# Rope scores of the decode streams in one single-pass product, keys and queries split into parts

## The reference, cut to what matters

```python
s = jnp.einsum('bqhc,bkc->bhqk', q_lat, ckv) + jnp.einsum('bqhr,bkr->bhqk', q_pe, kpe)
s = s.astype(jnp.float32) * MLA_SCALE
s = jnp.where(mask[None, None], s, jnp.finfo(jnp.float32).min)
p = jax.nn.softmax(s, axis=-1).astype(ckv.dtype)
```

## Time and profile before

| | |
|---|---|
| median of the runs | 2899.72 us |
| the profiled execution, its own time | 2900.53 us |
| its span | 2898.7 us |
| TensorE busy | 2745.8 us, 95% |
| VectorE busy | 1249.7 us, 43% |
| ScalarE busy | 888.6 us, 31% |
| GpSimd busy | 401.1 us, 14% |
| mean granted clock of TensorE | 0.981 |

### The profile page before, as it was taken

How to read it: one execution, slowest core, us unless ns; L and a number is a source line. 1 busy time by engine, 2 the same in 40 slices (tenths; PEclk the granted TensorE clock), 3 DMA queues, 4 the chain that set the end, 5 groups by cost and what they waited for, 6 DMA issues and landing times.

```text
span 2898.7 us, 45136 instructions
## 1 busy us (share of the span) xinstructions
PE 2745.8 (95%) x18648; PEld 2623.7 (91%) x18648; DVE 1249.7 (43%) x1695; ACT 888.6 (31%) x1182; POOL 401.1 (14%) x378
## 2 busy tenths in 40 slices
PE   6999999998998999999999999999989989999997
PEld 6999999895678899999989999999856888999997
DVE  3333333645765633333363323354466736332334
ACT  4221223415543422122332212233264424221222
POOL 0110011102135011001101001110122440100110
PEclk9999999999999999999999999999999999999998
DMA  3223223320015222321322222232101152222222
GB/s 112 73 62 88 82 56 89 80 53 10 18 27 97 59 73 62 89 82 56 89 59 72 66 80 79 57 100 76 27 7 31 37 102 59 72 66 80 78 58 75
DMA packets 367939, 191.19 MB, mean 66 GB/s; under 512 B 36477, under 2 KB 363472, under 8 KB 367822
## 3 DMA queue, kind: packets, MB, share of 16 engines
q1 hardware_dynamic: 363822, 179.07, 23.2%
q0 software_dynamic: 4000, 10.47, 1.4%
HBM read 183.58 MB, written 5.93 MB: 65 GB/s over the span
## 4 chain that ended last, share of the span: by engine, by line
PE 86%; DVE 6%; ACT 3%; issue 2%; POOL 2%; SPq 0%; DMA 0%; ACTq 0%; DVEq 0%; POOLq 0%
PE ps L584 25%; PE ps L586 25%; PE ps L585 25%; PE ps L819 2%; ACT w L1249 1%; PE ps L828 1%; POOL css L2467 1%; DVE w L1705 1%; PE ps L879 1%; DVE y L1794 1%; PE ps L947 1%; POOL ss L2467 1%; PE ps L861 1%; DVE at L1976 1%; PE ps L925 1%
## 5 line engine op out<-in xcount | busy, mean ns | idle before, releaser
L584 PE MATMUL ps<-xh,w 128*128 128x320 f32 x3456 | 1084.0, 314 | 56.9 <-DVE xl L1773 18.1
L585 PE MATMUL ps<-xl,w 128*128 128x320 f32 x3456 | 1077.4, 312 | 0.0
L586 PE MATMUL ps<-xh,w 128*128 128x320 f32 x3456 | 1077.3, 312 | 0.0
L584 PEld LDWEIGHTS ps<-xh,w 128*128 128x128 f32 x3456 | 657.5, 190 | 68.6 <-DVE xl L1773 25.3
L585 PEld LDWEIGHTS ps<-xl,w 128*128 128x128 f32 x3456 | 657.5, 190 | 0.3
L586 PEld LDWEIGHTS ps<-xh,w 128*128 128x128 f32 x3456 | 657.2, 190 | 0.0
L1705 DVE TENSOR_TENSOR w<-raw,w 128x2048 fp32r<-128x2048 f32 x180 | 418.5, 2325 | 426.7 <-ACT w L1249 426.7
L1249 ACT ACTIVATE w<-raw 128x2048 fp32r<-128x2048 f32 x181 | 345.2, 1907 | 483.2 <-PE ps L586 438.3
L584 PE MATMUL ps<-hh,w 128*128 128x320 f32 x1408 | 437.4, 311 | 1.0 <-DVE w L1705 1.0
L585 PE MATMUL ps<-hl,w 128*128 128x320 f32 x1408 | 435.1, 309 | 0.0
L586 PE MATMUL ps<-hh,w 128*128 128x320 f32 x1408 | 435.1, 309 | 0.0
(11 more groups left out here) (351 smaller groups left out, 2652.5 us busy)
## 6 DMA issues: line engine op xcount, KB each, us to landing
raw<-in_w_ffn_in_dram SPq DMA_DIRECT2D x178, 512.0 KB
raw<-in_w_ffn_out_dram SPq DMA_DIRECT2D x64, 384.0 KB
raw<-in_w_ffn_out_dram SPq DMA_DIRECT2D x64, 320.0 KB
raw<-in_w_in_dram SPq DMA_DIRECT2D x38, 512.0 KB
raw<-in_w_out_dram SPq DMA_DIRECT2D x16, 512.0 KB
out_dram<-xio SPq DMA_DIRECT2D x5, 512.0 KB, 3.1
xio<-in_x_prompt_dram SPq DMA_DIRECT2D x1, 2048.0 KB
y<-in_cache_ckv_dram POOLq DMA_DIRECT2D x8, 256.0 KB, 3.2
```

What stands on the lines that cost most here:

```text
L584: pe.matmul(out, wh, xh, start=first, stop=False)
L585: pe.matmul(out, wh, xl, start=False, stop=False)
L586: return pe.matmul(out, wl, xh, start=False, stop=last)
```

## The change

The rope product of the streams is computed in the 4-byte format that TensorE reads in one pass (`F32R` in the code), with keys and queries split in a high part (the value rounded to that format) and a low part (what is left). The parts stand below each other in the contracted rows, so that one product adds up three: high key times high query, low key times high query, high key times low query.

- Rows 0 to 31, 32 to 63 and 64 to 95 of KPT hold the high, the low and again the high part of the cached rope keys; QPE holds high, high and low of the queries; KN, now 96 rows, holds the new keys as KPT does.
- ScalarE, per stream: it copies the high rope keys first (`rope_hi`), then the latent keys, then copies the high part a second time, from its own result (`ct_sb`). VectorE computes the low part (`stream_rope_low`, `rope_lo`).
- ScalarE, per head: two copies of the rope queries instead of one. VectorE computes the low part (`latent_low`, `ql_lo`), and what reuses PSUM bank 2 waits for `ql_lo` instead of `ql_sb`.
- `pair_keys` and its first copy stand one step later, at 4h + 1, and on TensorE behind the transposes.
- Two zeroing instructions less per layer, since only rows 96 to 127 are left to clear. Two semaphores are merged into others (`y_stored` into `ml_stored`, `setup_ps` into `xio_ps`).

```diff
         def pair_keys(l, pair):
             if pair:
-                pe.wait_ge(*ql_sb.nth(l, 2 * pair - 1))
+                pe.wait_ge(*ql_lo.nth(l, 2 * pair - 1))
...
             pe.wait_ge(*ct_sb.nth(l, b))
+            pe.wait_ge(*rope_lo.nth(l, b + 1))
...
-            qn = QPE[0:ROPE, b, :, :].rearrange("c h t -> c (h t)")
+            qn = QPE[0:3 * ROPE, b, :, :].rearrange("c h t -> c (h t)")
...
-                if i == 0 and h % 2 and h + 1 < H:
-                    pair_keys(l, h // 2 + 1)
...
                 if n + 1 < NT:
                     attend_transpose(l, n + 1)
+                if i == 1 and h % 2 and h + 1 < H:
+                    pair_keys(l, h // 2 + 1)
...
-                run(QPE[0:ROPE, :, h, :], PS[0:ROPE, 2, P:2 * P].rearrange("p (b t) -> p b t", t=TS), ACT.Copy)\
-                    .then_inc(ql_sb.sem, 1)
+                for row in (0, ROPE):
+                    ins = run(QPE[row:row + ROPE, :, h, :], PS[0:ROPE, 2, P:2 * P].rearrange("p (b t) -> p b t", t=TS),
+                              ACT.Copy)
+                ins.then_inc(ql_sb.sem, 1)
...
+                run(KPT[0:ROPE, b % 2, 0:PAST], PS[0:ROPE, 1, :], ACT.Copy).then_inc(rope_hi.sem, 1)
                 run(CT[:, b % 2, :], PS[:, 0, :], ACT.Copy)
-                run(KPT[0:ROPE, b % 2, 0:PAST], PS[0:ROPE, 1, :], ACT.Copy).then_inc(ct_sb.sem, 1)
+                act.wait_ge(*rope_hi.nth(l, b))
+                run(KPT[2 * ROPE:3 * ROPE, b % 2, 0:PAST], KPT[0:ROPE, b % 2, 0:PAST].bitcast(F32), ACT.Copy)\
+                    .then_inc(ct_sb.sem, 1)
...
+            def latent_low(h):
+                dve.wait_ge(*ql_sb.nth(l, h))
+                V.tensor_tensor(QPE[2 * ROPE:3 * ROPE, :, h, :], PS[0:ROPE, 2, P:2 * P].rearrange("p (b t) -> p b t", t=TS),
+                                QPE[0:ROPE, :, h, :].bitcast(F32), ALU.subtract).then_inc(ql_lo.sem, 1)
...
+                if n % PT_ == 1:
+                    latent_low(n // PT_)
                 if n >= 3:
                     normalise(n - 3)
                 if n == NT - 3:
-                    V.memset(KPT[ROPE:64, :, 0:PAST], 0.0)
-                    V.memset(KPT[64:P, :, 0:PAST], 0.0)
+                    V.memset(KPT[3 * ROPE:P, :, 0:PAST].bitcast(F32), 0.0)
...
+            def stream_rope_low(b):
+                dve.wait_ge(*rope_hi.nth(l, b))
+                V.tensor_tensor(KPT[ROPE:2 * ROPE, b % 2, 0:PAST], PS[0:ROPE, 1, :],
+                                KPT[0:ROPE, b % 2, 0:PAST].bitcast(F32), ALU.subtract).then_inc(rope_lo.sem, 1)
...
+            dve.wait_ge(*kn_sb.nth(l, 0))
+            V.tensor_tensor(KN[ROPE:2 * ROPE, :], KPER[NOPE:QK, TP:T], KN[2 * ROPE:3 * ROPE, :].bitcast(F32), ALU.subtract)\
+                .then_inc(rope_lo.sem, 1)
+            stream_rope_low(0)
             stream_maximum(0)
...
                 for k in range(early):
+                    if k == early - 1 and b + 2 < NSEQ:
+                        stream_rope_low(b + 2)
                     level(m + k)
```

More of the change, by code:

```diff
@@ L185, in encoder @@
     SELG = tile(ctx, "selg", [P, 2, P])
+    s_w = ExitStack()
+    KPT = tile(s_w, "kpt", [P, 2, T], F32R)
+    s_w.close()
     GB = tile(ctx, "gb", [P, 2, T])
@@ L260, in encoder @@
     QLAT = tile(s_w, "qlat", [P, NSEQ, H, TS])
-    QPE = tile(s_w, "qpe", [P, NSEQ, H, TS])
+    QPE = tile(s_w, "qpe", [P, NSEQ, H, TS], F32R)
     CTOK = tile(s_w, "ctok", [P, TILES, KVL])
@@ L277, in encoder @@
     OLAT = tile(s_w, "olat", [P, H, P])
-    KN = tile(s_w, "kn", [ROPE, P])
+    KN = tile(s_w, "kn", [3 * ROPE, P], F32R)
     tile(s_w, "gap_mx", [P, 608])
@@ L281, in encoder @@
     s_w.close()
-    ROPET, SWAP, PAIR, KPT = UB[NOPE:P, 0, :], UB[0:QK, 1, 0:P], UB[NOPE:P, 1, P:P + ROPE], GB
+    ROPET, SWAP, PAIR = UB[NOPE:P, 0, :], UB[0:QK, 1, 0:P], UB[NOPE:P, 1, P:P + ROPE]
     SC, DROP = PB[0:NSEQ * 3, 0, :], KPER[0:MH, :]
@@ L320, in encoder @@
     setup_in = sem("setup_in")
-    setup_ps, setup_sb = sem("setup_ps"), sem("setup_sb")
+    setup_sb = sem("setup_sb")
     xio_ps, xio_sb = sem("xio_ps"), sem("xio_sb")
@@ L358, in encoder @@
     ct_ps, ct_sb = event("ct_ps", NSEQ), event("ct_sb", NSEQ)
+    rope_hi, rope_lo, ql_lo = event("rope_hi", NSEQ), event("rope_lo", NSEQ + 1), event("ql_lo", H)
     ss_ps, snm_sb, sexp_sb = event("ss_ps", NSEQ), event("snm_sb", NSEQ), event("sexp_sb", NSEQ)
@@ L395, in encoder @@
     ml_stored = sem("ml_stored")
-    y_stored = sem("y_stored")
     act_chain, dve_chain, pool_chain = sem("act_chain"), sem("dve_chain"), sem("pool_chain")
@@ L572, in _ @@
             dst = O["y_prompt"][0, t * P:(t + 1) * P, :] if t < PT_ else O["y_sample"].rearrange("b t f -> (b t) f")
-            sp.dma_start(dst, XIO[:, t, :]).then_inc(y_stored, 16)
-        sp.wait_ge(y_stored, 16 * TILES)
+            sp.dma_start(dst, XIO[:, t, :]).then_inc(ml_stored, 16)
         sp.wait_ge(stored, 16 * LAYER_STORES * LAYERS)
         sp.wait_ge(cn_stored, 32 * LAYERS)
-        sp.wait_ge(ml_stored, 256 * LAYERS)
+        sp.wait_ge(ml_stored, 256 * LAYERS + 16 * TILES)
     @block.tensor
@@ L843, in head_latents @@
             if h:
-                pe.wait_ge(*ql_sb.nth(l, h - 1))
+                pe.wait_ge(*ql_lo.nth(l, h - 1))
             if h % 2 and h > 2:
@@ L885, in pair_output @@
             pe.wait_ge(*on_sb.nth(l, 8 * pair + 7))
-            pe.wait_ge(*ql_sb.nth(l, min(2 * pair + 2, H - 1)))
+            pe.wait_ge(*ql_lo.nth(l, min(2 * pair + 2, H - 1)))
             for t in range(PT_):
@@ L909, in stream_keys @@
                 pe.wait_ge(*ct_sb.nth(l, b - 1))
+                pe.wait_ge(*rope_lo.nth(l, b))
             for k in range(4):
@@ L1189, in _ @@
         pe.transpose(PS[:, 0, 96:146], PROW[0:50, 1, :], IDENT[0:50, 0:50])
-        pe.matmul(PS[:, 1, 0:LAYERS * DK], ONES[0:1, :], HROW[:, :], start=True, stop=True).then_inc(setup_ps, 1)
+        pe.matmul(PS[:, 1, 0:LAYERS * DK], ONES[0:1, :], HROW[:, :], start=True, stop=True).then_inc(xio_ps, 1)
         pe.wait_ge(setup_sb, 1)
@@ L1557, in mla @@
             stream_keys(0)
-            run(KN[:, :], KPER[NOPE:QK, TP:T], ACT.Copy).then_inc(kn_sb.sem, 1)
+            for row in (0, 2 * ROPE):
+                ins = run(KN[row:row + ROPE, :], KPER[NOPE:QK, TP:T], ACT.Copy)
+            ins.then_inc(kn_sb.sem, 1)
             pair_output(H // 2 - 1)
@@ L1672, in _ @@
         for c in range(KD):
-            act.wait_ge(xio_ps, c + 1)
+            act.wait_ge(xio_ps, c + 2)
             run(X[:, c, :], psf[:, (c % 4) * 1024:(c % 4) * 1024 + T], ACT.Copy).then_inc(xio_sb, 1)
@@ L1693, in _ @@
         for t in range(TILES):
-            act.wait_ge(xio_ps, KD + t + 1)
+            act.wait_ge(xio_ps, KD + t + 2)
             run(XIO[:, t, :], psf[:, (t % 4) * 1024:(t % 4) * 1024 + D], ACT.Copy).then_inc(xio_sb, 1)
@@ L1900, in mla @@
             R_, S_ = slice(NOPE, QK), slice(QK, P)
-            V.memset(QPE[ROPE:64, :, :, :], 0.0)
-            V.memset(QPE[64:P, :, :, :], 0.0)
+            V.memset(QPE[3 * ROPE:P, :, :, :].bitcast(F32), 0.0)
             V.tensor_copy(CNT[:, :, :].rearrange("p c (b r) -> p c b r", r=3), EXTS[:, :, :, TS:TS + 3])\
@@ L2098, in mla @@
             level(1)
+            stream_rope_low(1)
             stream_maximum(1)
@@ L2267, in _ @@
         V.memset(HB[:, 0, 4:6], 1.0).then_inc(dve_setup, 1)
-        dve.wait_ge(setup_ps, 1)
+        dve.wait_ge(xio_ps, 1)
         V.tensor_copy(PAR[:, :], PS[:, 0, 0:PAR.shape[1]]).then_inc(dve_setup, 1)
```

## The result

The changed kernel took 2927.6 us (median of 6 runs, 2917.05 to 2932.32), the kernel before beside it 2899.47 us (6 runs, 2898.8 to 2904.17). The medians differ by 28.1 us. The ratio, which is not formed from the medians, is 1.0087 (some 25 us), with a 95% interval of 1.007 to 1.0103: slower. The forecast was 2908 (2893 to 2914), 9 us more than before. The direction was right and the size a third of what came; the median lies outside the range. The profiled execution of the changed kernel took 2921.44 us, span 2919.6; of before it was 2900.53.

The account below looks back on a forecast made before the run. TensorE was taken as fullest engine (busy 95%), with VectorE's queue blocking able to cost in full. Per layer, streams -2.1 and attention +6.65 gave +4.5, for two layers +9.1: 2899.7 + 9.1 = 2908.8, stated as 2908, range 2893 to 2914.

Parts of the forecast that it names:

- The mechanism: Attention: latent_low blocks VectorE's queue behind max(4h + 1) for at least an exponential and three ScalarE copies.
- head 5: Attention: VectorE free 1.8 us later, moved key copy late, scores(24) 2.4 us late; net +1.65 us.
- The signs that were named: One-record rope product, next 0.22 us later; VectorE idle over 1 us per subtraction; key-copy waits; 1.8 us before stream 0.
- head 2: Attention: subtraction ends 1.45 us late, max(10) and the exponential 1.4 us late; net +1.35 us.
- the sum over the attention's heads: Attention: delays of heads 1 to 7 added up, +6.65 us per layer.
- the bound of 11.6: Attention: upper limit in us per layer, seven heads times the largest head cost, 1.65.
- heads 3 and 4: Attention: +0.8 us together; head 3 costs 0.95, but the 2.07 us stall shortens and the slow stretch behind it goes.
- a wait given back: Attention, head 5: of the old 1.29 us idle before the next key copy, 0.75 us is regained.
- The border: Last attention scores to stream 0's scores: start 1.9 us late, waiting for VectorE's gate multiplication and two low parts.
- The streams: Streams' scores: shorter products save 0.80 us each, less waits for low parts and copies; net -2.1 us per layer.
- D: Rival: half speed behind new stalls before scores(24) and stream 0, 6 us more, 2914 to 2915; chance 0.10.
- A: The forecast itself: VectorE blocking outweighs the streams' gain, +9 us, 2903 to 2914; chance 0.45.

Follow-up runs that it names:

- e9: e7 with one ScalarE copy for both high query parts, and the waits for a stream's low part and zeroed PNEW placed later; 2893.6 us, ratio 0.998.
- e4: The changed kernel with the pair keys and their first copy back at step 4h; 2917.1 us, ratio 1.005.
- e2: The changed kernel with VectorE's latent_low one step later, behind max(4h + 2); 2900.86 us, ratio to before 0.9998.
- e3: The changed kernel with one exact query copy per head, GpSimd splitting all heads at once, pair keys at their old place; 2905.2 us, ratio 1.0015.
- e10: The changed kernel run once more, nothing altered; 2928.98 us (4 runs), ratio to before 1.0101.
- e6: The changed kernel with eight spin products filling TensorE's wait for stream 0's low part; 2924.65 us, ratio to before 1.0088.
- e5: e2 with the gate multiplication ahead of the last three normalise and KN's copies ahead of stream 0's keys; 2900.28 us, ratio to before 1.0007.
- e7: e5 with stream 3's low part one level step sooner, ahead of the two scalings; 2895.14 us, ratio 0.9982.
- e8: The kernel before with stream 0's scores also waiting for the HGG gate multiplication; 2900.48 us, ratio 1.0004.

## Why the prediction was wrong

- **The mechanism was right.** VectorE stands still behind max(4h + 1) until ScalarE has run the exponential and three copies. Predicted was VectorE free 1.8 us later in head 5; there the wait is 1.67 us and the subtraction 0.28 (0.25 assumed), and the eight waits are 1.8 us on average. The signs that were named came as well: waits of over 1 us ahead of every subtraction, waits for the key copy at the first scores of heads 2, 4 and 6 (0.83, 0.73 and 1.63 us), 1.84 us ahead of stream 0. One did not come in the form named: the new rope product is one record, but what follows starts 0.62 us later and not 0.22. Only both products together show the saving, 1.16 us instead of 1.72. In head 2 the division and max(10) came 1.6 us later against the head's first scores, predicted 1.45 and 1.4.
- **The step that failed is the sum over the attention's heads**, "1.0 + 1.35 + 0.8 + 1.65 + 1.35 + 0.5 = 6.65 us per layer". It measured 11.8, just above the bound of 11.6. By the distances of the heads' first scores: head 0 +0.4 (taken as nothing; with one ScalarE copy instead of two, in e9, it is gone, so it is the price of the second copy), head 1 +1.4, head 2 +1.6, heads 3 and 4 +1.9 (0.8), head 5 +4.4 (1.65), head 6 +1.0 (1.35), head 7 +1.1 (0.5). Head 5 alone is over half of the miss. Its own chain came as worked out: the maximum to the key copy, and scores(24) 2.7 us late where 2.4 was said. I then took 0.75 off for a wait given back, of which only 0.2 came (head 6's wait for its key copy, 1.29 before, is 1.09 now), and put in nothing for a stretch at the lower clock at the head's start, which cost 1.7 us. In e4 the same head has that stretch in layer 1 and not in layer 2, and takes 12.07 and 10.35 us. These rows and this window show it: the wait ahead of scores(20), the key copy's wait at scores(24), and the clock between.

```profile
750.49 0.73 PE L863 MATMUL ps<-kt,qt 128*128 128x128 f32 x2 [1.96 <-issue]
...
764.81 0.46 PE L863 MATMUL ps<-kt,qt 128*128 128x128 f32 x2 [1.63 <-ACT kt L1253]
```

```profile
750.00:755.00 5.00, 4.51 (x20) 3.65 (x21) 2.85 (x9) 2.25 (x7) 0.00 (x0) 0.66 0.01 3
```

- Heads 3 and 4: the stall of 2.07 did shrink, to 1.06, and the stretch of the earlier trace rows went with it, as assumed. But head 3 lost 2.8 where 0.95 was put: its successor's first scores now wait for the moved key copy. I had worked through one head of each kind and scaled the rest from them; the two heads with other work on VectorE between (gates and taps) were not like them. Of the 5.15 us missed per layer, 1.7 are the clock in head 5, 0.75 the wait that wasn't given back, 1.7 the heads that were scaled (1, 3, 4, 6 and 7 together), 0.4 head 0, and 0.5 small misses in the two heads that were worked in full.
- **The border**, predicted 1.9 late: 2.2 measured, wait 1.84.
- **The streams**, predicted to win 4.0 behind stream 0's start (2.1 net with the 1.9): 3.6 measured. Together that is 1.4 net where the clock holds, outside the bounds given for it, -6.4 to -2.1: their upper end was the forecast itself and left no room for a miss. Stream 0's four products are 0.77 us shorter (0.80). The second copy took 0.63 (0.57), the low part 0.68 (0.69), stream 3's scores waited 1.29 (1.3). These terms came out to a tenth. The 0.64 put on the rope product with the cached keys measured 0.56, the 0.16 on the one with the new keys 0.21.
- **The rivals.** D, the clock, was set against the forecast as another case, at 0.10. It was no alternative to A but an addition to it: the same waits that A is made of are what it needs. Behind the 1.84 to 1.95 us waits at stream 0, six of the ten profiled layers (after, e2, e3, e4, e10) fell to the lower clock, at 2.4 to 8.7 us each where the price given was 1.5. The two layers of e2 had the 1.84 us wait and no stretch. The layers with a shorter wait or none there had no such stretch at the streams' start. The waits that grew inside the attention are followed by it too: 1.96 us ahead of scores(20), in both layers of both profiled executions of the changed kernel.
- The Trainium skill's rule on idle gaps ("TensorE: Matmul & The Clock Gate", section "Why this matters for your kernels") points the right way, but the gaps that it names are longer than any of these, and here gaps of 1.8 to 2.0 us were followed by the lower clock; the measurement decides.
- The chances (slower 0.55) stood on the right side. The range was too narrow since its upper end added no clock and took the heads at their forecast, though the bound for them, 11.6, stood in the text: with it the sum was 2900 + 2 x 9.5 = 2919.
- **The miss, added up.** 9.1 us were forecast. The attention brings 10.3 more (5.15 per layer), the border and the streams 1.4, the clock at stream 0 2.6 or 5.0 (one layer or both). That makes 23.4 or 25.8 of the medians' 28.1; the rest is not placed, and of the size of what executions differ by elsewhere.

What stays open: how much of the median's 28 us is the clock at stream 0 (the two traces say 2.6 and 5, the timing of e6 says 3 with an uncertainty as large), why the same wait is followed by the lower clock in some executions and not in others, and what starts the stretch in e5.

## What to carry to other kernels

An instruction put into an in-order queue costs from the moment at which it reaches the head of it until its input is there, and all behind it pays; so put it where its input is already made (here one step later, worth 27 us in sixteen waits and the clock behind them, for a subtraction of 0.28 us). When a loop has eight rounds with other work in between, walk through each of them, and carry the delay from one to the next, instead of scaling from two. And where a forecast for a kernel like this one is made of waits of about 2 us on TensorE, the lower clock behind them belongs in the sum and not among the rivals.

## What the runs showed of the hardware

- TensorE's granted clock fell to half, 1.2 of 2.4 GHz, behind waits of 1.84 and 1.95 us at stream 0 in some layers of some executions and not in others (changed kernel: three of four; e2: none of two), for 7 us in the changed kernel, 10 us in e3 and 24 us in e4. In the attention it fell for 3.4 us behind 2.07 us (before) and 1.96 us (changed kernel); such a stretch cost 1.7 us (e4, head 5, layer 1 against 2). Behind 1.05 us (e5, e7), 0.79 us (e8) and with the wait filled by spins (e6) it stayed at 1.00 at that place.
- It also fell in e5 with TensorE busy 5.06 to 5.64 of 6 us ahead of it and no wait above 0.39 us, for 20 and 30 us.
- A ScalarE copy of 64 rows x 128 took 0.25 us (e9), as long as one of 32 rows; two of 32 rows took 0.53. So 32 more rows cost nothing there, and a second instruction costs 0.28.
- From the start of stream 0's first product to that of the new-key products it was 1.72 us and is 1.16 (793.64 to 794.80): the single-pass rope product over 512 columns saves 0.56. All four products took 2.26 and take 1.49 us. A VectorE subtraction of 32x512 took 0.68, of 32x128 0.28.
